# Attention steps of a residual block: both heads of a pair in one step, the division by the sum on ScalarE

## The reference

```python
# branch A, per query chunk, 128 keys
m = jnp.maximum(jnp.max(scores, axis=-1, keepdims=True), sink)
p = jnp.exp(scores - m)
probs = p / (jnp.sum(p, axis=-1, keepdims=True) + jnp.exp(sink - m))
out = jnp.einsum('bnkgqs,bnskd->bnqkgd', probs, vb)
# branch B, per query chunk, 576 keys
sc = jnp.einsum('bqhd,bkhd->bhqk', q_blk, k_blk) * scale + bias[None]
p = jax.nn.softmax(sc, axis=-1)
return jnp.einsum('bhqk,bkhd->bqhd', p, v_blk)
```

## Time and profile before

| | |
|---|---|
| median of 3 runs | 3795.68 us (3791.32 to 3795.94) |
| the profiled execution | time 3796.18 us, span 3794.4 us |
| TensorE busy | 3667.2 us, 97% of the span |
| DVE busy | 2380.1 us, 63% |
| ScalarE busy | 1368.3 us, 36% |
| GpSimd busy | 2026.4 us, 53% |
| mean granted TensorE clock | 0.988 of 2.4 GHz |

### The profile page before, as it was taken

How to read it: one execution, slowest core, us unless ns; L and a number is a source line. 1 busy time by engine, 2 the same in 40 slices (tenths; PEclk the granted TensorE clock), 3 DMA queues, 4 the chain that set the end, 5 groups by cost and what they waited for, 6 DMA issues and landing times.

```text
span 3794.4 us, 51599 instructions
## 1 busy us (share of the span) xinstructions
PE 3667.2 (97%) x20069; PEld 3270.2 (86%) x20069; DVE 2380.1 (63%) x4102; ACT 1368.3 (36%) x1718; POOL 2026.4 (53%) x696
## 2 busy tenths in 40 slices
PE   7999999999999999989899999999989999999999
PEld 5666767777778887878899999999989999999999
DVE  5444445555557413999766666654447777777773
ACT  5333344434332222232244434442323333333332
POOL 2222222222234443446576666667757777777774
PEclk9999999999999999999999999999999999999999
DMA  3322222222223433237789888899989999999993
GB/s 144 120 95 77 88 80 81 77 80 77 80 97 144 174 115 107 93 141 271 269 318 352 337 330 343 346 355 360 363 326 358 361 359 360 359 358 359 359 345 134
DMA packets 181577, 871.94 MB, mean 230 GB/s; under 512 B 15376, under 2 KB 68880, under 8 KB 90256
## 3 DMA queue, kind: packets, MB, share of 16 engines
q1 hardware_dynamic: 59376, 399.48, 28.4%
q0 software_dynamic: 46224, 336.61, 22.6%
q10 hardware_dynamic: 75792, 133.26, 9.7%
HBM read 805.30 MB, written 69.21 MB: 230 GB/s over the span
## 4 chain that ended last, share of the span: by engine, by line
PE 73%; DVE 19%; ACT 2%; issue 2%; DMA 1%; DVEq 1%; ACTq 0%; POOL 0%; SPq 0%
PE ps L1452 66%; DVE ps L1248 5%; PE ps L1683 2%; DVE psm L972 2%; PE ps L1534 2%; DVE expert_rows L1235 1%; DVE scores L976 1%; PE ps L1517 1%; PE ps L1526 1%; DVE h_dense L1372 1%; DMA g_dram<-gate_buf 1%; DVE cand L1207 1%; DVE cand L1209 1%; DVE tv_all L1198 1%; PE ps L1468 1%
## 5 line engine op out<-in xcount | busy, mean ns | idle before, releaser
L334 POOL TENSOR_TENSOR w_e_lo<-w_e_raw,w_e_hi 128x2048 fp32r<-128x2048 f32 x256 | 1183.6, 4626 | 537.4 <-ACT w_e_hi L683 536.1
L327 POOL TENSOR_TENSOR w_lo<-w_raw,w_hi 128x2048 fp32r<-128x2048 f32 x115 | 539.0, 4687 | 1088.6 <-ACT w_hi L394 1088.6
L1452 PE MATMUL ps<-sn_hi,w_e_hi 128*128 128x352 f32 x2048 | 673.0, 329 | 39.7 <-POOL w_e_lo L334 25.5
L1452 PE MATMUL ps<-act_hi,w_e_hi 128*128 128x352 f32 x2048 | 666.4, 325 | 20.9 <-DVE h_dense L1372 18.8
L1452 PE MATMUL ps<-act_lo,w_e_hi 128*128 128x352 f32 x2048 | 662.6, 324 | 0.0
L1452 PE MATMUL ps<-act_hi,w_e_lo 128*128 128x352 f32 x2048 | 661.5, 323 | 0.0
L1452 PE MATMUL ps<-sn_hi,w_e_lo 128*128 128x352 f32 x2048 | 660.5, 323 | 0.0
L1452 PE MATMUL ps<-sn_lo,w_e_hi 128*128 128x352 f32 x2048 | 660.0, 322 | 0.0
L683 ACT ACTIVATE w_e_hi<-w_e_raw 128x2048 fp32r<-128x2048 f32 x256 | 489.0, 1910 | 176.9 <-DMA w_e_raw<-w_stream 90.8
L1235 DVE SCALAR_TENSOR_TENSOR expert_rows<-expert_rows,ps 128x2048 f32<-128x2048 f32 x160 | 362.7, 2284 | 182.7 <-DMA expert_rows<-down_rows,idx 100.8
L1452 PE MATMUL ps<-xn_hi,w_hi 128*128 128x512 f32 x1088 | 448.5, 412 | 19.0 <-DVE xn_lo L886 19.0
(11 more groups left out here) (245 smaller groups left out, 5214.7 us busy)
## 6 DMA issues: line engine op xcount, KB each, us to landing
w_e_raw<-w_stream SPq DMA_DIRECT2D x256, 1024.0 KB, 7.4
w_raw<-w_stream SPq DMA_DIRECT2D x116, 1024.0 KB, 4.8
gel_dram<-gel_all ACTq DMA_DIRECT2D x32, 704.0 KB, 10.6
g_dram<-gate_buf ACTq DMA_DIRECT2D x11, 2048.0 KB, 13.0
gel_in<-gel_dram ACTq DMA_DIRECT2D x32, 704.0 KB, 5.9
g_exp<-g_dram ACTq DMA_DIRECT2D x32, 704.0 KB, 13.2
gate_dram<-g_raw ACTq DMA_DIRECT2D x32, 256.0 KB, 2.0
g_in<-gate_dram ACTq DMA_DIRECT2D x16, 512.0 KB, 6.2
```

The source lines that it names most:

```text
L327: nc.gpsimd.tensor_tensor(wlo[s][:, :], raw[s][:, :], whi[s][:, :].bitcast(F32), ALU.subtract).then_inc(lo_ready, 1)
L334: nc.gpsimd.tensor_tensor(e_lo[j % 4][:, :], e_raw[j % 4][:, :], e_hi[j % 3][:, :].bitcast(F32), ALU.subtract).then_inc(lo_ready, 1)
L1452: m = mm(ps[:, bank, 0:width], lhs[:, w], r, start=(n % (3 * per) == 0), stop=(n % (3 * per) == 3 * per - 1))
```

## The change

Ten steps per pair become six, behind matmul 12 + 33 k of the 192 (in the epilogue 12 + 26 k). Step k holds, for both heads, the scores of query tile k, the transposes of tile k - 1 and the values of tile k - 2; the value matmuls of the two heads alternate. Scores of the two heads go to neighbouring banks, and the two buffers for even and odd units become one for each head. DVE adds, takes the maximum, negates and takes reciprocals for both heads in one instruction each; the negation of kind A reads a new array `neg_sink`, filled once. The multiplication by the reciprocal goes to ScalarE, as a Copy with a scale from a column per head (`probs`). ScalarE's order is written anew: `exps`, `probs` and `probs_out` stand apart, `square` stands ahead of `hi`, `rsqrt_guess` behind it, and the bias rows of both heads of the next pair are loaded together after the last exponentials. The extras move to matmuls 78 and 165 (A), 78, 144 and 177 (B). The other stages are as they were.

```diff
-        bias = [at(f"bias{s}", 189 + 2 * s, S) for s in range(2)]
-        sc = [at(f"scores{s}", 193 + 2 * s, S) for s in range(2)]
-        pt = [at(f"probs_t{s}", 197 + 2 * s, S) for s in range(2)]
+        bias, sc, pt = (at(n, 189 + 4 * k, 2 * S)[:, :].rearrange("p (h c) -> p h c", h=2)
+                        for k, n in enumerate(["bias", "scores", "probs_t"]))
         rope_t = at("rope_t", 201, S)
...
+        neg_sink = at("neg_sink", 207.25, 16)
...
+
+            def exps(kind, i, a):
+
+                n = keys_of(kind, i) * P
+                act.wait_ge(s_sm, 4 * a + i + 1)
+                for hf in range(2):
+                    e = nc.scalar.activation(sc[:, hf, 0:n], sc[:, hf, 0:n], ACT.Exp, bias=negm[:, hf:hf + 1],
+                                             accum_out=psm[:, hf:hf + 1])
+                if kind == "A":
+                    for hf in range(2):
+                        e = nc.scalar.activation(esk[:, hf:hf + 1], cols[:, bass.ds(C_SINK + 2 * a + hf, 1)], ACT.Exp,
+                                                 bias=negm[:, hf:hf + 1])
+                e.then_inc(s_exp, 1)
+
+            def probs(kind, i, a):
+
+                n = keys_of(kind, i) * P
+                act.wait_ge(s_rcp, 4 * a + i + 1)
+                for hf in range(2):
+                    e = nc.scalar.activation(sc[:, hf, 0:n], sc[:, hf, 0:n], ACT.Copy, scale=rcp[:, hf:hf + 1])
+                e.then_inc(s_nrm, 1)
 
             def load_bias(head, slot):
-                act.dma_start(bias[slot][:, :], skewed(head)).then_inc(bias_in[slot], 16)
+                act.dma_start(bias[:, slot, :], skewed(head)).then_inc(bias_in[slot], 16)
 
             act.dma_start(cols[:, :], small).then_inc(s_cols, 16)
 
@@ -502,30 +513,33 @@
                 if not (isinstance(n, int) and n == 1):
                     take_gate(b - 1, 0, 2, 3 * n - 4, n - 2)
                 hi(b0, 1, i)
-                step("A", 0, a)
...
-                step("A", 1, a)
+                exps("A", 0, a)
+                probs("A", 0, a)
+                probs_out("A", 0, a)
                 act.wait_ge(att_ready, a + 1)
                 take(b, 1, q_st[:, :])
+                square(b, q_st[:, :])
                 hi(b0, 2, i)
-                square(b, q_st[:, :])
+                exps("A", 1, a)
+                probs("A", 1, a)
                 if isinstance(n, int):
                     spread_bias(2 * (n - 1))
-                step("A", 2, a)
-                step("A", 3, a)
-                rsqrt_guess(2 + n)
-                step("A", 4, a)
+                probs_out("A", 1, a)
+                exps("A", 2, a)
+                probs("A", 2, a)
                 take_gate(b + 1, 0, 0, 3 * n - 3, n - 1)
                 hi(b0, 3, i)
-                for k in (5, 6, 7):
-                    step("A", k, a)
+                rsqrt_guess(2 + n)
+                probs_out("A", 2, a)
+                exps("A", 3, a)
+                probs("A", 3, a)
+                if isinstance(n, int):
+                    spread_bias(2 * (n - 1) + 1)
+                probs_out("A", 3, a)
...
-                    load_bias(2 * (a - 8) + 1, 1)
-                step(kind, 1, a)
+                exps(kind, 0, a)
+                probs(kind, 0, a)
+                probs_out(kind, 0, a)
                 act.wait_ge(att_ready, a + 1)
                 take(b, 1, q_st[:, :])
+                square(b, q_st[:, :])
                 hi(b0, 2, i)
-                square(b, q_st[:, :])
-                step(kind, 2, a)
-                step(kind, 3, a)
-                rsqrt_guess(10 + 2 * (n - 8))
-                step(kind, 4, a)
+                exps(kind, 1, a)
+                probs(kind, 1, a)
+                probs_out(kind, 1, a)
+                exps(kind, 2, a)
+                probs(kind, 2, a)
                 take(b + 1, 0, k_st[:, :])
                 hi(b0, 3, i)
+                rsqrt_guess(10 + 2 * (n - 8))
                 square(b + 1, k_st[:, :])
-                step(kind, 5, a)
+                probs_out(kind, 2, a)
+                exps(kind, 3, a)
                 if kind == "A":
                     act.wait_ge(s_ext, 64)
-                load_bias(2 * (a - 7), 0)
-                step(kind, 6, a)
-                rsqrt_guess(11 + 2 * (n - 8))
-                step(kind, 7, a)
+                for hf in range(2):
+                    load_bias(2 * (a - 7) + hf, hf)
+                probs(kind, 3, a)
...
             hi(B_EPI, 1)
-            load_bias(15, 1)
-            for k in (0, 1, 2, 3):
-                step("B", k, 15)
+            exps("B", 0, 15)
+            probs("B", 0, 15)
+            probs_out("B", 0, 15)
+            exps("B", 1, 15)
             take_gate(B_EPI, 1, 0, 29, 15)
+            probs("B", 1, 15)
             hi(B_EPI, 2)
-            for k in (4, 5, 6):
-                step("B", k, 15)
+            probs_out("B", 1, 15)
+            exps("B", 2, 15)
+            probs("B", 2, 15)
+            probs_out("B", 2, 15)
             take_gate(B_EPI + 1, 0, 1, 30, 7)
+            exps("B", 3, 15)
+            probs("B", 3, 15)
             hi(B_EPI, 3)
-            for k in (7, 8, 9):
-                step("B", k, 15)
+            probs_out("B", 3, 15)
...
-            def step(kind, k, a):
-
-                if k >= 8:
-                    return
-                n, r = min(k % 4 + 1, 2 if kind == "A" else 4) * P, k % 2
-                if k >= 2:
-                    v.wait_ge(s_tr, 8 * a + k - 1)
-                if kind == "B" and k % 4 == 0:
-                    v.wait_ge(bias_in[k // 4], 16 * (a - 7))
-
-                    tail = bias[k // 4][:, 512 - P:512]
-                    vec.tensor_tensor(tail, tail, mask_a[:, P:2 * P], ALU.add)
+            def step(kind, i, a):
+
+                n = keys_of(kind, i) * P
+                if i >= 1:
+                    v.wait_ge(s_tr, 4 * a + i)
+                both = lambda line: line.rearrange("p (o c) -> p o c", o=1)
+                if kind == "B" and i == 0:
+                    for hf in range(2):
+                        v.wait_ge(bias_in[hf], 16 * (a - 7))
+                    tail = bias[:, :, 512 - P:512]
+                    vec.tensor_tensor(tail, tail, both(mask_a[:, P:2 * P]).to_broadcast([P, 2, P]), ALU.add)
                     v.drain()
-                v.wait_ge(s_qk, 8 * a + k + 1)
-                b = mask_a[:, 256 - n:256] if kind == "A" else bias[k // 4][:, 512 - n:512]
-                vec.tensor_tensor(sc[r][:, 0:n], ps[:, SC + r, 0:n], b, ALU.add)
-                v.drain()
-                vec.reduce_max(mx[:, r:r + 1], sc[r][:, 0:n], AX)
+                v.wait_ge(s_qk, 4 * a + i + 1)
+                b = both(mask_a[:, 256 - n:256]).to_broadcast([P, 2, n]) if kind == "A" else bias[:, :, 512 - n:512]
+                vec.tensor_tensor(sc[:, :, 0:n], ps[:, SC:SC + 2, 0:n], b, ALU.add)
+                v.drain()
+                vec.reduce_max(mx[:, :], sc[:, :, 0:n], AX)
                 v.drain()
                 if kind == "A":
-                    c = C_SINK + 2 * a + k // 4
-                    vec.tensor_scalar(negm[:, r:r + 1], mx[:, r:r + 1], cols[:, bass.ds(c, 1)], -1.0,
-                                      ALU.max, ALU.mult).then_inc(s_sm, 1)
+                    vec.scalar_tensor_tensor(out=negm[:, :], in0=mx[:, :], scalar=-1.0, in1=neg_sink[:, bass.ds(2 * a, 2)],
+                                             op0=ALU.mult, op1=ALU.min).then_inc(s_sm, 1)
                 else:
-                    vec.tensor_scalar(negm[:, r:r + 1], mx[:, r:r + 1], -1.0, None, ALU.mult).then_inc(s_sm, 1)
-                v.wait_ge(s_exp, 8 * a + k + 1)
+                    vec.tensor_scalar(negm[:, :], mx[:, :], -1.0, None, ALU.mult).then_inc(s_sm, 1)
+                v.wait_ge(s_exp, 4 * a + i + 1)
                 if kind == "A":
-                    vec.tensor_tensor(psm[:, r:r + 1], psm[:, r:r + 1], esk[:, r:r + 1], ALU.add)
+                    vec.tensor_tensor(psm[:, :], psm[:, :], esk[:, :], ALU.add)
                     v.drain()
-                vec.reciprocal(rcp[:, r:r + 1], psm[:, r:r + 1])
-                v.drain()
-                vec.tensor_scalar(sc[r][:, 0:n], sc[r][:, 0:n], rcp[:, r:r + 1], None, ALU.mult).then_inc(s_nrm, 1)
+                vec.reciprocal(rcp[:, :], psm[:, :]).then_inc(s_rcp, 1)
...
-                for k in range(4):
+                for k in range(3):
                     step("A", k, a)
                 v.drain()
                 mean_square(2 + n)
-                step("A", 4, a)
+                step("A", 3, a)
                 normed(2 + n, q_st[:, :], qscaled[:, 0:1])
-                for k in (5, 6, 7):
-                    step("A", k, a)
                 rope(2 + n, q_st[:, :], q_st[:, :])
...
-                if k < 8:
-                    hf, i, ts = where(k)
-                    rows = slice(HD * hf, HD * hf + HD)
-                    if k >= 2:
-                        pe.wait_ge(s_sm, 8 * a + k - 1)
```

(52 more changed lines are left out.)

56 lines of the change are left out of this document (18 added, 38 removed).

## The result

| | before | after |
|---|---|---|
| median | 3793.97 us (3791.32 to 3795.94, 4 runs) | 3664.03 us (3661.62 to 3668.47, 4 runs) |
| span of the profiled execution | 3794.4 us | 3659.8 us |
| stage with attention | 993.7 us | 865.4 us |
| TensorE busy | 3667.2 us | 3559.4 us |
| DVE busy | 2380.1 us | 2228.7 us |

What follows compares the result with a forecast made beforehand. The prediction took TensorE's matmul stream and what interrupts it as the bound. It summed -44.8 - 27.4 + 8.5 + 0.4 - 4.8 = -68.1 us to 3728 us, range 3683 to 3762.

Steps and rivals of the forecast that it cites:

- step 1: TensorE inserts: six per pair instead of ten save four fixed parts of 0.70 us, -44.8 us; two heads priced serially.
- full overlap: Scores and values of the two heads in an insert: both array halves fully overlap, the gain-side bound of step 1.
- second rival: Halves overlap by neighbouring passes in scores and values: 32 us more gain, 3696 us; overlap, whole or part, chance 0.34.
- Step 2: Division leaves DVE for ScalarE: all 27.4 us of probability-transpose waits go, if no new ones come.
- Step 3: A pairs, second transpose insert: GpSimd holds the sum of exponentials, TensorE waits 1.05 us, eight times, +8.5 us.
- Steps 4 and 5: B pairs wait nothing; in the epilogue take_gate ahead of exps(3) makes probabilities late, +0.4 us.
- Step 6: A pairs: reduced clock behind waits goes, granted clock 1.00 through the stage, -4.8 us, with 0 as the other end.
- The drain at each head: Third rival, scores and values: each switch between heads' halves drains like a change of kind, 3807 us; chance 0.03.
- the late ScalarE queue: Fourth rival: ScalarE's in-order queue makes steps 1 to 3 wait, 3755 to 3770 us; chance 0.15 with small switching prices.

Runs made afterwards that it cites:

- e6b: e6 with kind A's sum of exponentials as a tensor_scalar with a column instead of two tensors: 3758.31 us, stage 958.2 us.
- e9: e3 with both heads' scores and values computed on half 0 of the array, so serially, in six inserts: 3709.08 us.
- e3: The changed kernel with kind A's negation and sum each as two one-tensor instructions with a column operand: 3647.75 us, stage 852.0 us.
- e7: e3 with steps 1 to 3 each cut into two inserts, scores first, transposes and values six matmuls later: 3658.77 us.
- e6: The kernel before, ten inserts of one head, with only the division moved to ScalarE: 3788.32 us, stage 990.4 us.
- e5: The changed kernel with the division back on DVE, as two multiplications by a column behind the reciprocal: 3667.04 us.
- e4: The changed kernel with square behind hi again on ScalarE, as before the change: 3662.78 us, stage 860.2 us.
- e2: The changed kernel with head 1's scores moved behind the transposes in the steps that have transposes: 3715.80 us.

## Why the prediction missed by half

The stage, taken apart by pairs of kernels. The last two steps differ in one thing each. e6b and e9 differ in more, the places of the extras and the order on ScalarE and DVE, but in neither does a matmul wait in a pair, so only the inserts tell them apart on TensorE.

| term | forecast | measured | between |
|---|---|---|---|
| waits and lower clock gone | -27.4 - 4.8 = -32.2 | -35.5 | before, e6b |
| ten inserts become six, heads serial | -44.8 | -48.6 | e6b, e9 |
| both halves at the same time | 0 | -57.6 | e9, e3 |
| new wait in each A pair | +8.5 | +13.4 | e3, after |
| sum | -68.5 | -128.3 | before, after |

(The forecast's +0.4 of the epilogue is left out of the table. In e3 and e9 the negation and the sum of kind A are in their one-tensor form; the price of the held form is the last term.)

**The step that failed** is the last sentences of step 1: "For the two heads of one insert ... I take that, since it is the only neighbour case that the trace has." The neighbours of rows 4 use the same half of the array, and the new ones use different halves; the nearest row was not near. It priced the second head's scores and values at their full time; the runs show it at nothing, 57.6 us (e9 against e3), of the 60 by which the forecast fell short in the stage. The prediction held full overlap as a bound, "with half of everything, some 3675", but wrote its second rival down to 32 us by a model of single passes, with nothing at one tile because a weight load (184 ns) is longer than a pass. Weight loads don't stand in the way: at one tile, both heads take 0.42 us to the next matmul after (693.20 to 693.62), as one head did before (677.27 to 677.68 in rows 4, 0.41), and 0.64 in e9 (716.83 to 717.47). The Trainium skill, page TensorEngine Tiling (Array Packing), section Tiling Modes, says that different tiles load and multiply in parallel and only a change of mode drains; e9 against e3 agrees with the first, 57.6 us, and e7 with the second, since there the stops cost little and the changes between kinds stayed. The prediction took a gain of only 32 us from that rule.

**Step 1, fixed part.** Right in kind, mis-sized by 3.8 us: 48.6 against 44.8, 3.04 us a pair instead of 2.8. A part of it is a term that the prediction left out: of the extras, one in each A pair and three in each B pair now share their place with an insert, and stops that fall away have a price too (e7). The epilogue, which has no extras, gained 2.94 (48.29 in e6b, 45.35 in e9), an A pair 3.03 and a B pair 3.06.

**Step 2, waits.** Right in that they go and in what holds DVE; wrong in what removes them. In B it is the division's move: 0.6 us a pair, in the order of before (e6) and in the new one (e5 gives 0.61 back). In A, where nearly all of the time lay, the move alone removes nothing, because the sum stays held (e6: 23 waits, 24.2 us, about three a pair); after has one a pair. Two of three went with the new order, in which a chain has 33 matmuls of the stream instead of 18; ScalarE's order changed with it, and no run parts the two. The prediction credited the division with all 27.4 us.

**Step 3, new wait.** Right in place, cause and count (the second insert with transposes, eight times, GpSimd's end), short by 0.5 us each: 1.59 instead of 1.05. It is step 1's error again. The transposes were put behind 0.85 us of scores; the scores take 0.43 less, so TensorE arrives 0.43 earlier. 1.05 + 0.43 = 1.48, and GpSimd ended 0.14 later than forecast (7.74 us from the take instead of 7.6). e4 confirms the other side: GpSimd 0.67 earlier, wait 0.65 less.

**Steps 4 and 5.** No B pair waits, as forecast, though not for the whole reason given: the negation of a B pair's first step is held 3.8 us (last section), which step 4 left out. Its probabilities are done at 700.40 and the transposes start at 701.96, so 1.6 us were to spare. In the epilogue no matmul waits for ScalarE, where +0.4 us was expected.

**Step 6, clock.** Forecast 1.00 behind waits near 1 us; the waits are 1.6 and the clock stayed at 1.00 in the A pairs of after all the same, while before it fell behind 1.5 us in three of eight (rows 8), and in e2 behind 1.6 us in six of eight. The result is right, the reason (a shorter wait) is not: after and e2 have the same wait of 1.6 us at the same place. What decides it is open, and that no pair of after lost clock may be luck.

**The rivals.** The drain at each head is out, the late ScalarE queue too: its waits are in A only and are GpSimd's. Chance 0.34 for the overlap was too little, and the range ended at 3683 although the text's own bound of the disputed term was 3675. Even that bound lies 11 us over the result: waits and fixed parts were each short by 3 to 4 us, and some 6 lie behind the stage, against 4.9 of the new wait the other way.

## What to carry to other kernels

Matmuls on different halves of TensorE's array (rows 0 to 63 and 64 to 127 as the contraction, or the same halves of the columns as the output), issued one after the other and equally large, cost here as much as one of them, in float32 and with their weight loads: price them as one, keep them neighbours, and don't take matmuls of one half as a bound. Count changes between kinds of matmul, not stops. When DVE is held while GpSimd works, first make its small operations one element per partition with a column as the other operand; that was worth 13 us here (e3), and 32 in the order of before with the division moved too (e6b against e6), while moving the division alone was worth 3.
